# A two-model fp32 chain on one Trainium2 core: index scores and selection rounds moved within the last block's input projection

## What is computed

```
h = rms(x); proj = h @ w_in
u, q, k, v, qi, ki, wi, gates = split(proj)          # 512,512,64,64,256,64,4,2048 columns
y_ssm = s5(u)                                        # diagonal state-space scan, in four chunks of 8 groups
q, k, ki = rms of each head
iscore = sum over 4 heads of relu(qi . ki) * wi      # causal; rows in blocks of 128
keep the 128 keys of highest iscore in each row
y_att = softmax(q . k over the kept keys) @ v
x = x + (sigmoid(g_ssm) * (y_ssm @ W1) + sigmoid(g_att) * (y_att @ W2)) @ w_out
x = x + swiglu feed-forward
```

## Time and profile before

| | us |
|---|---|
| median of 3 runs | 3150.65 (3150.64 to 3152.95) |
| the profiled execution | 3156.53 |
| its span in the trace | 3154.5 |
| input projection of the last block, first unit's end to first chunk | 2418.9 to 2512.0 |
| four chunks | 2512.0 to 2593.2 |

### The profile page before, as it was taken

How to read it: one execution, slowest core, us unless ns; L and a number is a source line. 1 busy time by engine, 2 the same in 40 slices (tenths; PEclk the granted TensorE clock), 3 DMA queues, 4 the chain that set the end, 5 groups by cost and what they waited for, 6 DMA issues and landing times.

```text
span 3154.5 us, 57568 instructions
## 1 busy us (share of the span) xinstructions
PE 3068.6 (97%) x21924; PEld 2778.8 (88%) x21924; DVE 2144.6 (68%) x3084; ACT 1216.4 (39%) x1827; POOL 1350.7 (43%) x960
## 2 busy tenths in 40 slices
PE   7999999999999999999999999999999998999999
PEld 7999999899999999999999877788888776688998
DVE  7888664477588885888754567523235678768885
ACT  5333444322344444434344333332324444344442
POOL 3444432233544444444443233644465563444443
PEclk9999999999999999999999999999999999999999
DMA  4333322134333332333223234333333533233333
GB/s 132 95 96 97 97 76 61 51 93 132 97 91 93 97 103 86 90 100 100 86 74 81 54 88 135 104 96 107 93 92 93 107 101 132 70 95 100 100 100 97
DMA packets 546219, 299.10 MB, mean 95 GB/s; under 512 B 24368, under 2 KB 529840, under 8 KB 545904
## 3 DMA queue, kind: packets, MB, share of 16 engines
q1 hardware_dynamic: 515728, 259.86, 28.9%
q10 hardware_dynamic: 30304, 36.65, 3.7%
HBM read 278.37 MB, written 16.91 MB: 94 GB/s over the span
## 4 chain that ended last, share of the span: by engine, by line
PE 58%; issue 21%; POOL 8%; DVE 8%; DMA 2%; ACT 1%; ACTq 1%; POOLq 0%; DVEq 0%; SPq 0%
PE pair L749 21%; PE aux L814 21%; PE pair L751 15%; POOL wl L610 8%; DMA raw<-ffn_w_gu 1%; DVE R L1955 1%; DVE tmp L1965 1%; DMA raw<-w_ffn_gate 0%; ACTq L1748 0%; DVE al L1970 0%; DVE hT L1894 0%; DVE TL L1961 0%; DVE tmp L1997 0%; DVE R L1954 0%; DVE xl L2204 0%
## 5 line engine op out<-in xcount | busy, mean ns | idle before, releaser
L610 POOL TENSOR_TENSOR wl<-raw,wh 128x256 fp32r<-128x256 f32 (+3 forms) x848 | 1170.8, 1400 | 1773.5 <-ACT wh L1355 1325.7
L1355 ACT ACTIVATE wh<-raw 128x1024 fp32r<-128x1024 f32 (+4 forms) x613 | 511.5, 835 | 463.2 <-DMA raw<-ffn_w_gu 245.6
L751 PE MATMUL pair<-xh,wh 128*128 128x264 f32 x1344 | 251.7, 296 | 16.9 <-DVE xl L2204 11.1
L1894 DVE SCALAR_TENSOR_TENSOR hT<-pair,hT 128x528 f32 (+3 forms) x208 | 145.0, 697 | 170.4 <-PE pair L749 126.5
L749 PE MATMUL pair<-xh,wh 128*128 128x512 f32 x776 | 238.7, 407 | 0.5 <-DVE gst L1870 0.4
L751 PE MATMUL pair<-xl,wh 128*128 128x264 f32 x1344 | 238.1, 286 | 0.0
L751 PE MATMUL pair<-xh,wl 128*128 128x264 f32 x1344 | 231.7, 285 | 2.2 <-POOL wl L610 2.2
L749 PE MATMUL pair<-xl,wh 128*128 128x512 f32 x776 | 230.0, 396 | 0.0
L749 PE MATMUL pair<-xh,wl 128*128 128x512 f32 x776 | 226.6, 395 | 0.3 <-POOL wl L610 0.3
L751 PE MATMUL pair<-ah,wh 128*128 128x264 f32 x1256 | 211.8, 286 | 5.0 <-ACT wh L1355 2.9
L751 PEld LDWEIGHTS pair<-xh,wh 128*128 128x128 f32 x1344 | 194.6, 190 | 23.5 <-ACT wh L1355 9.5
(11 more groups left out here) (432 smaller groups left out, 6535.4 us busy)
## 6 DMA issues: line engine op xcount, KB each, us to landing
raw<-ffn_w_gu SPq DMA_DIRECT2D x176, 512.0 KB, 3.8
raw<-w_in SPq DMA_DIRECT2D x103, 512.0 KB, 3.8
raw<-ffn_w_down SPq DMA_DIRECT2D x96, 256.0 KB, 2.9
raw<-ffn_w_down SPq DMA_DIRECT2D x32, 384.0 KB, 3.3
raw<-w_out SPq DMA_DIRECT2D x24, 512.0 KB, 3.7
raw<-w_ffn_gate SPq DMA_DIRECT2D x22, 512.0 KB, 4.7
raw<-w_ffn_up SPq DMA_DIRECT2D x22, 512.0 KB, 3.7
gate_scratch<-gst ACTq DMA_DIRECT2D x32, 256.0 KB, 2.1
```

Of the source, the lines that this page charges most:

```text
L610: ins = nc.gpsimd.tensor_tensor(wl[:, k % SPL, n], raw[:, k % SPL, n], wh[:, k % SPL, n].bitcast(F32), ALU.subtract)
L751: mm = nc.tensor.matmul(pp[:, h, 0:th], wk, x[:, kk, t0 + h * th:t0 + (h + 1) * th], start=first, stop=last)
L1355: nc.scalar.activation(wh[:, k % SPL, n0:n], raw[:, k % SPL, n0:n], ACT.Copy).then_inc(S["split_hi"], 1)
L1894: v.scalar_tensor_tensor(halves(hm, T // 2), psum_pair(k, T // 2), factor, halves(hm, T // 2), ALU.mult, ALU.add).then_inc(S["evacuated"], ...
```

## The change

IN2 becomes ki, v/wi, qi, qi, k, then u and q as before. ki's norm therefore comes two units earlier. Scores 0 and 1 are issued by PE behind unit 4, 3 and 4 behind unit 5, 6 and 7 behind unit 6, 9 and 10 behind unit 7; scores 2, 5, 8 and 11 stand inside the gemm of units 5, 6, 7 and 8, behind its first eight matmuls. ACT's relus and DVE's index_score calls get new places. The selection starts at j = 6: 3, 3, 3, 4, 5, 4 rounds for j = 6 to 11 (22), none at j = 12, and 2, 2, 2, 1 in the chunks (7). 29 rounds lie before the attention as before.

```diff
--- before.py
+++ after.py
@@ -407,8 +407,12 @@
 
             return (N_META, SEQ) if l == DEPTH - 1 else (0, T1)
 
-        IN2 = (10, 11, 12, 9, 8, 0, 1, 2, 3, 4, 5, 6, 7)
-        KI, VW, K2, U0, Q0 = 2, 3, 4, 5, 9
+        IN2 = (12, 9, 10, 11, 8, 0, 1, 2, 3, 4, 5, 6, 7)
+        KI, VW, QI, K2, U0, Q0 = 0, 1, 2, 4, 5, 9
+
+        INDEX_IN = {5: (2,), 6: (5,), 7: (8,), 8: (11,)}
+        INDEX_END = {4: (0, 1), 5: (3, 4), 6: (6, 7), 7: (9, 10)}
+        PICKS_IN, PICKS_CHUNK = {6: 3, 7: 3, 8: 3, 9: 4, 10: 5, 11: 4}, (2, 2, 2, 1)
         EARLY = 2
         LATE = EARLY + 7
         MORE2 = [(U_GATE2 + g, KD) for g in range(LATE, 16)] + [(U_GLU + j, 4) for j in range(4)] + [(U_PROJ2 + m, 4) for m in range(KD - 2)]
@@ -1223,6 +1227,8 @@
 
                 i, h = n // 4 + 1, n % 4
                 st, sz = TT2[i]
+                if n == 0:
+                    pe.wait_ge(S["evacuated"], U(None, U_IN2 + QI + 1) + 1 + PAIRS)
                 pe.wait_ge(S["n2_done"], 1)
                 if n >= 2:
                     pe.wait_ge(S["rel_done"], n - 1)
@@ -1251,7 +1257,8 @@
             for j in range(13 + EARLY):
                 gemm(None, U_IN2 + j, KD, (xh, xl), th,
                      ready=(lambda kk: (S["x_ready"], x2 - KD + kk + 1)) if j == 0 else None,
-                     sums=((norm_sum_2, (aux45, SQA, SQ2[1])), (norm_sum_2, (aux67, A32, US))) if j == 0 else None)
+                     sums=((norm_sum_2, (aux45, SQA, SQ2[1])), (norm_sum_2, (aux67, A32, US))) if j == 0 else None,
+                     inside=(lambda: [index_scores(n) for n in INDEX_IN[j]]) if j in INDEX_IN else None)
                 if j == KI + 1:
                     norm2(0)
                 if j == VW + 1:
@@ -1261,9 +1268,8 @@
                     mm.then_inc(S["vt_done"], 1)
                 if j == K2 + 1:
                     norm2(1)
-                if 5 <= j < 11:
-                    index_scores(2 * (j - 5))
-                    index_scores(2 * (j - 5) + 1)
+                for n in INDEX_END.get(j, ()):
+                    index_scores(n)
                 if j == 8:
                     rows_of_chunk(0)
                 if j == 9:
@@ -1755,8 +1761,12 @@
                                      scale=con[:, C_PH + 4:C_PH + 5]).then_inc(S["act_step"], 1)
 
             for j in range(13):
+                for n in INDEX_IN.get(j, ()):
+                    relu(n)
                 if j in (KI, K2) or j >= U0:
                     act.wait_ge(S["evacuated"], U(None, U_IN2 + j) + 1 + PAIRS)
+                for n in INDEX_END.get(j, ())[:1]:
+                    relu(n)
                 if U0 <= j < U0 + 4:
                     permute(j - U0)
                 if j == KI:
@@ -1768,9 +1778,8 @@
                     rms2(0)
                 if j == K2 + 1:
                     rms2(1)
-                if 5 <= j < 11:
-                    relu(2 * (j - 5))
-                    relu(2 * (j - 5) + 1)
+                for n in INDEX_END.get(j, ())[1:]:
+                    relu(n)
                 if j == 8:
                     rows_of_chunk(0)
                 if j == 9:
@@ -2576,6 +2585,8 @@
             m8 = tmp[:, 2112:2624]
             cidx = con[:, C_CIDX:C_CIDX + NCH].unsqueeze(1).broadcast_to([P, 8, NCH])
             for j in range(13):
+                for n in INDEX_IN.get(j - 1, ()):
+                    index_score(n)
                 evac(None, U_IN2 + j, dsts[j], rstd2[:, :], th)
                 if j == 0:
                     inv_rms(n2 - 1, SEQ, rstd, n2 + 1)
@@ -2590,11 +2601,9 @@
                     v.tensor_copy(negq[0], causal).then_inc(S["negm_ok"], 1)
                 if j == 12:
                     norm2(1)
-                if 6 <= j < 12:
-                    index_score(2 * (j - 6))
-                    index_score(2 * (j - 6) + 1)
-                if j >= 8:
-                    pick(3)
+                for n in INDEX_END.get(j - 1, ()):
+                    index_score(n)
+                pick(PICKS_IN.get(j, 0))
             angles(0, (0,))
             gates(0, 1)
             dve.wait_ge(S["n2_rms"], 3)
@@ -2622,10 +2631,10 @@
                 gates(EARLY + 2 * b, EARLY + 2 * b + 1)
                 if b < 3:
                     angles(b + 1)
-                    pick(4)
+                    pick(PICKS_CHUNK[b])
                     gates(EARLY + 2 * b + 1, EARLY + 2 * b + 2)
                 else:
-                    pick(2)
+                    pick(PICKS_CHUNK[b])
 
             def more2(n, slot):
                 for q in PLAN2.ends(n, slot):
```

## The result

The changed kernel takes 3157.55 us (median of 20 runs, 3150.93 to 3164.06) against 3151.38 us for the kernel before in the same comparison (20 runs, 3146.26 to 3156.78). The ratio is 1.0021, 95% interval 1.0015 to 1.0027: slower by 6.6 us by the ratio. Timed again beside other kernels (11 runs) it was 1.0011, interval 1.0002 to 1.0021, which is 3.5 us; the two medians of that comparison, 3159.25 and 3153.38 us, lie 5.9 us apart. I had forecast 2.8 us faster.

The account below looks back on a forecast made before the run. PE, busy 97%, was taken to bound the kernel. A gain of 7.7 us in the chunks less 4.85 lost in the input projection gave 2.8 us gained, from 3150.65 to 3147.9 us; range 3144 to 3154.5.

Parts of the forecast that it names:

- Chunk 0: First attention chunk: without three rounds ahead of the angles, PE's 1.95 us wait and 1.61 us slow clock go, 3.6 gained.
- Chunk 2: Third chunk: two fewer rounds cut PE's wait from 4.11 to 1.6 us; 4.1 us gained with the clock staying up.
- The waits: Input projection: PE waits for relus through evacuation, addition, relu; 1.4 us at score 7, 1.5 at score 10.
- the 1.05 of the bound: DVE's score additions behind units 6 and 7 could take 1.05 instead of 0.48 us, adding 1.2 us of loss.
- the rule that I had weighed: Two-input DVE and POOL operations on SBUF exclude each other; additions held while POOL splits, raising losses to about 6 us.
- The wait for the square: Behind unit 10, q_sums waits 1.45 us for ACT's square, behind the DMA issues of responses; 1.1 us lost.
- PE's work is the same, in other places: Input projection: PE's work only moves; four single scores inside gemms cost 0.2 to 0.4 us in entries and exits.
- The bound on the clock: Input projection: each wait of 1.4 to 1.6 us can bring slow clock, 1.6 us a time, three times, +4.8.
- Rival (a): Waits at score 7, score 10, q_sums and chunk 2 cost the clock: 3.6 us slower, 3154.2; chance 0.17.
- the prediction's own worst case of 3155.4: Slow clock behind the score waits plus additions held by POOL: 3155.4 us.
- (b): Input projection's waits are hidden because PE's scores run further ahead of ACT and DVE: 3143.5 us; chance 0.12.
- (c): Chunk 0 keeps its wait, set by ACT's table loads and root; price 3.6 us, 3151.5; chance 0.13.

Follow-up runs that it names:

- old_rounds: Changed kernel with the selection rounds put back (3 behind each of units 8 to 12; 4, 4, 4, 2 in chunks): input projection 111.45 us, chunks 77.91.
- before_again: The kernel before, unchanged, run once more for a second trace: input projection and chunks together 177.8 us.
- after_timed: The changed kernel a third time, timed beside versions that move only rounds: ratio 1.0011 to the kernel before; the two stages together 180.1 us.
- after_again: The changed kernel, unchanged, run once more for a second trace: input projection and chunks together 185.6 us, 10.24 us at 1.2 GHz.
- adds_ahead: Changed kernel with DVE's additions of scores 0, 3, 6, 9 put ahead of the next unit's evacuation: input projection 105.27 us.
- early_rounds: Kernel before with only rounds moved (4, 4, 5, 5, 4 behind units 7 to 11; 2, 2, 2, 1 in chunks): ratio 0.9981, again 0.9979.
- rows_same: Kernel before with heads 1 and 3 given the row offset of heads 0 and 2: input projection 100.73 us.
- pairs_back: Changed kernel with scores in pairs again behind units 4 to 9, none inside a gemm: ratio 0.9998 to the kernel before.

## Why the prediction was wrong

- **Chunk 0: the forecast came, its reason is only half of it.** The wait of 1.95 us went; from the swap matmul to the outputs (2521.58 to 2524.79) it takes 3.2 us, what that stretch takes at full clock, where it took 4.92. But in old_rounds the three rounds are back behind unit 12, and chunk 0 has no wait there either. The difference is in the angles behind the rounds. In before an operation of POOL runs beside them, and one of them takes 2.52 us and ends 0.3 us after POOL's:

```profile
2507.98 2.52 DVE L2433 TENSOR_SCALAR tmp<-tmp 128x512 f32<-128x512 f32 x1
2507.35 2.86 POOL L688 TENSOR_TENSOR con<-con 128x1024 f32<-128x1024 f32 x1
```

  In old_rounds POOL's operation is over before the angles start, and the same one takes 0.43 us:

```profile
2517.84 0.43 DVE L2442 TENSOR_SCALAR tmp<-tmp 128x512 f32<-128x512 f32 x1
2513.53 2.83 POOL L692 TENSOR_TENSOR con<-con 128x1024 f32<-128x1024 f32 x1
```

  In after it is the other way round: one angle operation takes 2.76 us beside POOL, but no round stands ahead of it, and there is no wait. By these traces the wait of before needed both, the rounds (2.95 us) and the held angle (2.1 us); the prediction took it for the rounds' alone. The 1.61 us of slow clock that I counted as gained here belonged to one execution: in before_again the wait of 1.69 us in chunk 0 is followed by the full clock (3.34 us from the swap matmul to the outputs).
- **Chunk 2: right in size.** Forecast was a wait of 1.6 us and a clock that stays up; 1.27 us were left in the first trace, 1.29 in after_timed and 2.50 in after_again, and no trace of a kernel with seven rounds in the chunks has the slow clock there. All four chunks were to gain 7.7 us; between the first traces they gained 8.0, between the means of all traces (80.8 and 73.5) 7.3.
- **The waits: right in cause and nearly in size.** Score 7 was to go 1.9 us after PE came to the scores and went 1.98 after (2453.34 to 2455.32); score 10 2.1 and 2.23 (2463.18 to 2465.41). The timeline of DVE and of ACT has the chain as written, evacuation, addition 3, relu 5:

```profile
2453.51 0.69 DVE L1879 TENSOR_TENSOR R<-pair,rstd 128x512 f32<-128x512 f32 x1 [7.34 <-PE pair L753]
2454.12 0.47 DVE L2549 SCALAR_TENSOR_TENSOR negt<-tmp,R,negt 128x256 f32<-128x256 f32 x1
```

```profile
2454.69 0.49 ACT L1733 ACTIVATE tmp<-aux 128x384 f32<-128x384 f32 x1 [5.10 <-DVE negt L2549]
```

  The additions took 0.47 and 0.61 us, not the 1.05 of the bound: POOL ran nothing beside them, so the rule that I had weighed was not put to the test at these additions. An operation of DVE that is held while one of POOL runs is what the rows under chunk 0 show, where I had not looked for it. The wait for the square was 1.70 us (1.45 forecast).
- **"PE's work is the same, in other places": wrong, and this is the step that failed.** I priced a split pair as two halves with 0.1 us for each entry and exit, 0.2 to 0.4 us in all. A pair was one price for two scores because they ran at the same time. The four scores inside gemms cost 0.84, 1.02, 1.26 and 1.25 us (start to start across the first sixteen matmuls, less the 1.86 of eight), 4.4 us in all, while the pairs that are left behind units 4 to 7 cost 3.4 us even without waits (adds_ahead), against 5.1 for the six pairs of before: 2.6 us lost, where I had 0.3. The three pairs with a wait between their scores cost 4.9 us more than in adds_ahead, of which I had 3.2, the waits alone. With 1.35 for the square and 0.3 for ki's norm that is 9.2 of the 9.4 us.
- **The bound on the clock: right in kind and in price, too low in chance.** Rival (a), that the new waits cost the clock, is true in some executions: of the four traces that have all the new waits, after_again and old_rounds show 10.24 us of slow clock behind them, after and after_timed none. It had a chance of 0.17. The failed step alone turns 2.8 us gained into about 2.1 lost (9.4 in the input projection against 7.3 in the chunks); on the 3151.38 us of before that is 3153.5, still inside the range of 3144 to 3154.5. The slow clock, worth 4.7 us where it comes and 4.8 by (a)'s price, is what the traces offer for the rest of the way to the median of 3157.55; how often it comes in executions without a trace is not known. The range also ended below the prediction's own worst case of 3155.4. Rivals (b) and (c) are refuted by L1236's waits and by chunk 0. The forecast of no change by more than 0.2% fails by a little in one comparison, 1.0021, and holds in the other, 1.0011.
- **The absolute number.** The kernel before was at 3151.38 us in the comparison and not at 3150.65; that is 0.7 of the 9.65 us by which the forecast of 3147.9 missed.

## What to carry to other kernels

Before a group of small matmuls is taken apart, look at their rows of the array: if a pair's price in the trace is that of one, it is one slot, and splitting it, or letting one of the two wait, buys the second slot anew. When the same handful of stages changes and the rest of the program is noise of several us, cut the traces at fixed instructions and compare stages, with the time at the lower clock beside them. And try each part of a change alone: here one part gained 0.2% (early_rounds) and both together lost 0.1 to 0.2%, so that the other cost 0.3 to 0.4%.

## What the runs showed that I had not expected

Two scores of 64 rows each run at the same time: 0.63 against 1.05 us (256 keys) and 1.06 against 1.92 us (512) for two, by nothing but their row offset. PE's waits of 3.83 to 4.11 us in chunk 2 had the lower clock at or behind them in all four traces that have them (before, before_again, rows_same, old_rounds), and those of 1.95 to 2.10 us were followed by it (before in chunk 0, adds_ahead, pairs_back). But a wait of 2.50 us in chunk 2 of after_again was not, nor was one of 1.69 us in chunk 0 of before_again; and those of 1.1 and 1.7 us in the input projection were followed by it in after_again and old_rounds and not in after and after_timed, though they stand in the same places there. So for waits of 1.1 to 2.5 us, what they cost beside themselves is not settled by their length. And two executions of one kernel differ by up to 7 us in the 2410 us ahead of the change, of which the slow stretches listed in the traces explain only a part.
